# Scores of the stick-breaking attention from rounded hi and lo parts instead of plain f32

## The reference

```python
z = jnp.einsum('bqhd,bkhd->bhqk', q_blk, k_pre).astype(jnp.float32)   # q is scaled by 128 ** -0.5
log_beta = jax.nn.log_sigmoid(z)
log_1m = jnp.where(causal, jax.nn.log_sigmoid(-z), 0.0)               # causal: key strictly before query
rest = lax.cumsum(log_1m, axis=3, reverse=True) - log_1m
a = jnp.where(causal, jnp.exp(log_beta + rest), 0.0)
outs.append(jnp.einsum('bhqk,bkhd->bqhd', a.astype(v.dtype), v_pre))
```

## Time and profile before

| | us |
|---|---|
| median of 3 runs (lowest, highest) | 2148.46 (2148.44, 2149.17) |
| profiled execution, its time | 2148.72 |
| profiled execution, span of the trace | 2146.8 |
| TensorE busy | 2138.7 |
| VectorE busy | 1192.1 |
| ScalarE busy | 1009.1 |

### The profile page before, as it was taken

How to read it: one execution, slowest core, us unless ns; L and a number is a source line. 1 busy time by engine, 2 the same in 40 slices (tenths; PEclk the granted TensorE clock), 3 DMA queues, 4 the chain that set the end, 5 groups by cost and what they waited for, 6 DMA issues and landing times.

```text
span 2146.8 us, 26768 instructions
## 1 busy us (share of the span) xinstructions
PE 2138.7 (100%) x9585; PEld 1776.4 (83%) x9585; DVE 1192.1 (56%) x1187; ACT 1009.1 (47%) x1157; POOL 39.0 (2%) x50
## 2 busy tenths in 40 slices
PE   9999999999999999999999999999999999999998
PEld 8888888888888888888888888888888888888887
DVE  5555555555555566566555656665555555554444
ACT  6444444444444455456544545554444444444343
POOL 0000000000000021000000000000000000000000
PEclk9999999999999999999999999999999999999999
DMA  8766677666666677765587766676676667665554
GB/s 304 252 215 211 212 224 222 209 213 196 226 216 214 211 269 238 239 210 188 176 283 243 233 207 187 200 241 215 209 232 215 212 211 226 221 212 191 194 187 157
DMA packets 182995, 468.15 MB, mean 218 GB/s; under 512 B 16784, under 2 KB 67344, under 8 KB 182800
## 3 DMA queue, kind: packets, MB, share of 16 engines
q1 hardware_dynamic: 180768, 459.87, 66.5%
q0 software_dynamic: 1728, 6.82, 0.9%
q10 hardware_dynamic: 432, 0.58, 0.1%
HBM read 439.41 MB, written 27.79 MB: 218 GB/s over the span
## 4 chain that ended last, share of the span: by engine, by line
PE 98%; DMA 1%; ACT 0%; issue 0%; DVE 0%; SPq 0%; POOLq 0%; DVEq 0%; POOL 0%
PE acc L1629 32%; PE acc L1631 32%; PE acc L1632 32%; DMA raw<-in_ffn_w_in 1%; DMA x_t<-in_x_cols 0%; ACT w_hi L622 0%; PE aux L1926 0%; PE aux L1899 0%; PE aux L1895 0%; PE aux L1894 0%; PE aux L1921 0%; PE aux L1922 0%; PE aux L1836 0%; DVE w_lo L1042 0%; ACT a_hi L640 0%
## 5 line engine op out<-in xcount | busy, mean ns | idle before, releaser
L1042 DVE TENSOR_TENSOR w_lo<-raw,w_hi 128x1024 fp32r<-128x1024 f32 x765 | 936.1, 1227 | 891.1 <-ACT w_hi L622 889.7
L622 ACT ACTIVATE w_hi<-raw 128x1024 fp32r<-128x1024 f32 x765 | 808.0, 1060 | 1048.1 <-PE acc L1632 1013.0
L1629 PE MATMUL acc<-w_hi,a_hi 128*128 128x512 f32 x1384 | 539.6, 390 | 0.1
L1631 PE MATMUL acc<-w_lo,a_hi 128*128 128x512 f32 x1384 | 539.0, 389 | 0.0
L1632 PE MATMUL acc<-w_hi,a_lo 128*128 128x512 f32 x1384 | 539.0, 389 | 0.0
L1629 PE MATMUL acc<-w_hi,b_hi 128*128 128x512 f32 x1216 | 475.0, 391 | 0.0
L1632 PE MATMUL acc<-w_hi,b_lo 128*128 128x512 f32 x1216 | 473.7, 390 | 0.0
L1631 PE MATMUL acc<-w_lo,b_hi 128*128 128x512 f32 x1216 | 473.6, 390 | 0.0
L1629 PEld LDWEIGHTS acc<-w_hi,a_hi 128*128 128x128 f32 x1384 | 259.9, 188 | 55.2 <-issue 1.6
L1632 PEld LDWEIGHTS acc<-w_hi,a_lo 128*128 128x128 f32 x1384 | 259.9, 188 | 53.7
L1631 PEld LDWEIGHTS acc<-w_lo,a_hi 128*128 128x128 f32 x1384 | 259.9, 188 | 53.5
(11 more groups left out here) (195 smaller groups left out, 689.3 us busy)
## 6 DMA issues: line engine op xcount, KB each, us to landing
raw<-in_ffn_w_in SPq DMA_DIRECT2D x349, 512.0 KB, 4.3
raw<-in_ffn_w_out SPq DMA_DIRECT2D x176, 512.0 KB, 4.2
raw<-in_w_mix_in SPq DMA_DIRECT2D x80, 512.0 KB, 4.4
raw<-in_w_ckv SPq DMA_DIRECT2D x64, 512.0 KB, 4.3
memq<-bounce SPq DMA_DIRECT2D x196, 128.0 KB, 3.8
bounce<-stage SPq DMA_DIRECT2D x37, 512.0 KB, 5.0
raw<-in_w_mix_out SPq DMA_DIRECT2D x32, 512.0 KB, 4.6
raw<-in_w_cq SPq DMA_DIRECT2D x32, 512.0 KB, 4.2
```

Of the source, the lines that this page charges most:

```text
L622: eng.activation(w_hi[:, u % RING], raw[:, u % RING], ACT.Copy).then_inc(w_hi_done, 1)
L1042: eng.tensor_tensor(w_lo[:, u % RING], raw[:, u % RING], w_hi[:, u % RING].bitcast(f32), ALU.subtract).then_inc(w_lo_done, 1)
L1629: eng.matmul(dst, x_hi[:, rows], w_hi[:, slot, i], start=start and i == 0, stop=False)
L1631: eng.matmul(dst, x_hi[:, rows], w_lo[:, slot, i], start=False, stop=False)
```

## The change

The scores are made from rounded parts, as the weight products are. Before pair c's scores, ScalarE copies the pair's q and k (4 blocks of 128 x 256, 1024 columns) into `zin_hi`, and VectorE subtracts into `zin_lo`. For pair 0 this is at u = 4 (ScalarE) and u = 6 (VectorE) of w_mix_in's chunk 8; for pairs 1 to 3 it is at u = 7 of w_ckv's chunk c - 1 on ScalarE, behind its copy of unit 7, and at u = 0 of chunk c on VectorE, behind its subtraction of unit 0. `zin_hi` lies where v of the first token tile was, `zin_lo` where v of the second was. Because `mem_v` overwrites that place from its chunk 3 on, VectorE waits there for the scores of pair 3. TensorE waits for `zin_lo` and makes three products in place of each plain one: 12 per pair, six with 256 and six with 128 columns.

```diff
@@ memory: over the second half of uv
+            sb("qk_t_and_u", [P, 2 * HEADS_B * TOK + W_GROUP], f32, region)
+            zin_hi = sb("zin_hi", [P, 2, 2, TOK], f32r, region)
+            sb("u_second", [P, W_GROUP], f32, region)
+            zin_lo = sb("zin_lo", [P, 2, 2, TOK], f32r, region)
...
+        def heads_qk(pair):
+            return qk_t[:].rearrange("p (s h) n -> p s h n", s=2)[:, :, 2 * pair:2 * pair + 2]
@@ ScalarE, w_mix_in
+                    if u == 4 and c == 8:
+                        eng.wait_ge(turned, number(TURNS, "qk", 1) + 1)
+                        eng.wait_ge(gv_lo_done, 2)
+                        eng.activation(zin_hi[:], heads_qk(0), ACT.Copy).then_inc(zin_hi_done, 1)
@@ ScalarE, w_ckv
+                    if u == 7 and c < 3:
+                        eng.wait_ge(turned, number(TURNS, "qk", 3) + 1)
+                        eng.wait_ge(aux_full, AUX.index(f"z{c}") + 1)
+                        eng.activation(zin_hi[:], heads_qk(c + 1), ACT.Copy).then_inc(zin_hi_done, 1)
@@ VectorE, w_mix_in
+                    if u == 6 and c == 8:
+                        eng.wait_ge(zin_hi_done, 1)
+                        eng.tensor_tensor(zin_lo[:], heads_qk(0), zin_hi[:].bitcast(f32), ALU.subtract
+                                          ).then_inc(zin_lo_done, 1)
@@ VectorE, w_ckv
+                    if u == 0 and 1 <= c <= 3:
+                        eng.wait_ge(zin_hi_done, c + 1)
+                        eng.tensor_tensor(zin_lo[:], heads_qk(c), zin_hi[:].bitcast(f32), ALU.subtract
+                                          ).then_inc(zin_lo_done, 1)
...
                         if c <= 2:
                             eng.wait_ge(sent, 16 * number(TURNS, f"ya{c - 1}") + 16)
+                        if c == 3:
+                            eng.wait_ge(aux_full, AUX.index("z3") + 1)
                         values(first, (c - 1) % 2, "mem", mem_v[:, :, CH * (c - 1):CH * c])
@@ TensorE, w_ckv, u == 1 and c < 4
-                        if c % 2 == 0:
-                            eng.wait_ge(turned, number(TURNS, "qk", 3) + 1)
+                        eng.wait_ge(zin_lo_done, c + 1)
                         eng.wait_ge(aux_read, AUX.index(f"z{c}"))
                         for a in range(2):
-                            q_t, k_t = qk_t[:, 2 * c + a], qk_t[:, HEADS_B + 2 * c + a]
-                            eng.matmul(aux[:, a, 0:TOK], k_t[:, 0:P], q_t, start=True, stop=True)
-                            last = eng.matmul(aux[:, a, TOK:384], k_t[:, P:TOK], q_t[:, P:TOK],
-                                              start=True, stop=True)
+                            for keys, queries in ((slice(0, P), slice(0, TOK)), (slice(P, TOK), slice(P, TOK))):
+                                at = 0 if keys.start == 0 else TOK
+                                dst = aux[:, a, at:at + queries.stop - queries.start]
+                                eng.matmul(dst, zin_hi[:, 1, a, keys], zin_hi[:, 0, a, queries],
+                                           start=True, stop=False)
+                                eng.matmul(dst, zin_hi[:, 1, a, keys], zin_lo[:, 0, a, queries],
+                                           start=False, stop=False)
+                                last = eng.matmul(dst, zin_lo[:, 1, a, keys], zin_hi[:, 0, a, queries],
+                                                  start=False, stop=True)
                         last.then_inc(aux_full, 1)
```

More of the change, by code:

```diff
@@ L219, in encoder_block @@
         with ExitStack() as region:
+            sb("qk_t_and_u", [P, 2 * HEADS_B * TOK + W_GROUP], f32, region)
+            zin_hi = sb("zin_hi", [P, 2, 2, TOK], f32r, region)
+            sb("u_second", [P, W_GROUP], f32, region)
+            zin_lo = sb("zin_lo", [P, 2, 2, TOK], f32r, region)
+        with ExitStack() as region:
             qk_t = sb("qk_t", [P, 2 * HEADS_B, TOK], f32, region)
@@ L314, in encoder_block @@
         qk_done = sem("qk_done")
+        zin_hi_done = sem("zin_hi_done")
+        zin_lo_done = sem("zin_lo_done")
         z_done = sem("z_done")
```

## The result

| | before | after |
|---|---|---|
| median of 12 runs, us | 2148.50 | 2153.78 |
| lowest and highest | 2148.06, 2150.77 | 2153.26, 2154.19 |
| span of the profiled execution | 2146.8 | 2151.6 |

The kernel became 5.28 us slower; the ratio is 1.0024 with a 95% interval of 1.0015 to 1.0032. The forecast was 2154.0 (2154.0 - 2148.46 = 5.5 us slower).

A forecast was written before the change was run, and what follows sets the result against it. TensorE's issued work bounds the kernel (busy 2138.7 of 2146.8 us). Insertions 3.43 plus chunk 3's wait 2.05 make 5.48 us: 2154.2 on the profiled execution, 2154.0 on the runs' median; range 2150.7 to 2155.8.

The forecast's parts named there:

- The insertions: Chunks 0 to 2 of w_ckv: added copies and subtractions delay ex, so av starts 1.55, 2.64, 3.43 us late in all.
- The wait in chunk 3: VectorE's mem_v values wait for pair 3's scores, making z and sp_lo late; cum starts 2.05 us later.
- The block on TensorE: Each pair's scores: 12 rounded products take 1.44 us, +0.13 us; outside chunk 3 this hides in waits.
- The price of 0.12 us for a narrow product: Rounded 128-column product in the score block: 0.12 us taken, with 0.22 and 0.06 us as the alternatives.
- the total: Whole loss if a 128-column product costs 0.06 us: chunk 3's z comes 0.39 us earlier, total 5.1 us.
- The supply of weights: Weight units in chunk 3 stay supplied: unit 4's subtraction ends at 1031.4, TensorE comes to it at about 1034.
- The waits named as signs: TensorE waits in av of chunks 0, 1, 2 for ex (1.5, 1.0, 0.7 us), in chunk 3's cum for sp_lo (1.9).
- (a): Score block: rounded 128-column products cost as much as plain f32 ones, 0.22 us; +6.1 us, 2154.6; chance 0.22.
- (b): Added copies and subtractions are absorbed, only chunk 3's wait for the scores bites; 2.4 us, 2150.8; chance 0.12.
- (c): Only the added copies and subtractions bite, chunk 3's softplus having slack; 3.43 + 0.13 us, 2152.0; chance 0.09.
- (d): Not slower: score block cheap, no wait at av; -0.9 us, 2147.6, or +0.5 us, 2149.0; chance 0.09.
- (e): Late VectorE subtractions also starve the ring or a weight transfer; over 6.5 us, 2155.5; chance 0.07.

The follow-up runs named there:

- run 2: Changed kernel, but hi and lo parts of pairs 1 to 3 made at u = 5 of the chunk before; 2150.65 us, before 2148.43.
- run 3: Changed kernel with parts of pairs 1 to 3 made at u = 5 and chunk 3's mem_v values behind z; 2148.49 us, before 2148.43.
- run 5: Changed kernel, chunk 3's values behind z, VectorE's subtraction for pairs 1 to 3 behind ex at u = 1; 2149.53 us, before 2148.59.
- run 6: Changed kernel, chunk 3's values behind z, ScalarE's copy at u = 5, VectorE's subtraction left at u = 0; 2150.17 us, before 2148.59.
- run 1: Changed kernel, but chunk 3's mem_v values written behind the evacuation of z at u = 5; 2151.71 us, before 2148.43.
- run 7: As run 3, but the second key block takes all 256 queries, so all 12 products are 256 columns wide; 2148.77 us, before 2148.59.
- the better mix: As run 3, but 128-column products plain f32, only 256-column ones from rounded parts; 2147.95 us, before 2148.59; again 2147.97, before 2148.53.

## Why the prediction was right

**The insertions**, forecast 1.55, 2.64, 3.43 us by the end of chunks 0, 1, 2: measured 1.53, 2.66, 3.45. ex 1.83 us late was 1.85 (5.25 less 3.40). The first masks ended 20.10 us after the scores of pair 0 (970.06 - 949.96), exactly as worked out (970.83 - 950.73). Runs 2 and 3 show the cause: with the copies two units and the subtractions three units earlier, and in run 3 the values behind z, the same work costs nothing that can be measured. Runs 5 and 6 divide it, and in the traces both parts count: ScalarE's copy makes ex 0.71 us late, VectorE's subtraction 1.14. Alone they make the scores of pair 3 start 1.05 us late (run 5, masks slowed by 0.3 us included) and 1.33 (run 6), together 3.47 (run 1), which is 1.09 more than the sum. The room between masks and "av" in the three chunks before (0.46, 0.65, 1.11 us, less the 0.18 that a late operand costs) is free for each part alone and only once for both; that this makes all of the 1.09 is argued, not shown.

**The wait in chunk 3**, forecast 2.05: measured 1.86 in the trace (5.31 less 3.45), 1.87 in run 2 by itself, and 5.28 less 3.3 by run 1, about 2.0. The term was too large because the values started 1.53 us after the scores and not 1.70: the last product was issued 1.22 us after the first, not 1.32, and the release took 0.04 us, not 0.10. The 0.10 stood on no row; ScalarE's starts behind TensorE in the trace of before, 0.04 us after the product's end, would have given it. This is the largest error of the sum, 0.19 of 5.48 us.

**The block on TensorE**, forecast +0.13: from scores to "cum" of chunk 1, 12.27 us against 12.24, +0.03. The price of 0.12 us for a narrow product was the right one of the three, with weight loads 0.115 apart. Of the two figures that the prediction took from the Trainium skill, TensorE: Matmul & The Clock Gate, the 107 ns of the section LDWEIGHTS is near the trace's 0.115 us, and the 56 ns of the section Back-to-back issue gap is not. Of the 0.10 us too much, 0.06 are 12 products at 0.12 instead of 0.115; where the other 0.04 went is open. (One slip in the sum: six products at 0.06 instead of 0.12 us are 0.36 us, not 0.39; the total stays 5.1.)

**The supply of weights**, forecast untouched: no weight product waits in the stretch. The waits named as signs all came, somewhat shorter than named, since idle time is less than the loss: 1.29, 0.82 and 0.48 us for ex and 1.55 for sp_lo, where 1.5, 1.0, 0.7 and 1.9 were named. VectorE was idle 4.13 us before the values of chunk 3.

**Rivals.** (a) falls by the spacing of 0.115 us, where it asked for 0.22, and by run 7. (b) and (c) are each half of the truth: runs 2 and 1 are these cases made real, at +2.2 and +3.3 where 2.4 and 3.6 were worked out. (d) needed no late mask; the first masks ended at 970.06, and TensorE, which took 18.73 us from scores to "av" before, would have come at 949.96 + 18.73 = 968.69. (e) did not happen.

## What to carry to other kernels

When one engine is always busy, list for the stretch in question how early each hand-over comes, and put a new helper operation where its engine idles between two steps of the same chain, not behind the next unit of its routine work: the same copies, subtractions and values cost 5.3 us in one place and nothing measurable in another (0.07 us in the traces). Storage that is free until a certain write makes that write wait for the last reader; move the write into the next gap before looking for other memory. Count weight loads before replacing f32 products by rounded parts: for 256 columns three rounded products took 0.35 us against 0.43 for the plain f32 one, for 128 columns 0.345 against 0.22. Even the better mix gains too little here (0.14 us a block) to show in the time.

## What the runs showed of the hardware that I had not expected

GpSimd's two masks of 256 columns took 1.09 us instead of 0.77 while a VectorE subtraction of two SBUF tiles ran (run 5), 0.3 us straight on the critical chain. And what the prediction had only assumed: a rounded product of 128 columns and one of 256 cost nearly the same where each has its own weight load: 12 products with half of them narrow and 12 wide ones differ by 0.06 us (run 7).
